# Down projection of the gated ConvFFN in a diffusion inference step: seven block products in place of eight

## The reference

```python
def conv_ffn(h, rows, cols, w_up, w_dw, b_dw, w_down):
    up = h @ w_up
    a, g = jnp.split(up, 2, axis=-1)
...
    g4 = lax.conv_general_dilated(g4, w_dw.reshape(3, 3, 1, D_FF).astype(g4.dtype), (1, 1), 'SAME',
                                  dimension_numbers=('NHWC', 'HWIO', 'NHWC'), feature_group_count=D_FF)
    g = g4.reshape(B, L, D_FF) + b_dw
    return (jax.nn.gelu(g) * a) @ w_down
...
    ffn = conv_ffn(h, rows, cols, p['w_up'], p['w_dw'], p['b_dw'], p['w_down'])
    x = layer_norm(ALPHA * x + g2[:, None, :] * ffn, p['ln2_g'], p['ln2_b'])
```

## Time and profile before

| | us |
|---|---|
| median of 3 runs | 1409.03 |
| lowest and highest | 1407.51, 1412.31 |
| the profiled execution: its own time | 1409.17 |
| its span from first to last instruction | 1407.4 |

### The profile page before, as it was taken

One profiled execution on the slowest core, in us unless ns is written; L12 is line 12 of the kernel. 1 busy time (PEld: TensorE's weight loads), 2 busy tenths in 40 slices (PEclk: granted clock), 3 DMA queues, 4 the chain that ended last, 5 costly groups with the idle time before them and its releaser, 6 DMA issues.

```text
span 1407.4 us, 22364 instructions
## 1 busy us (share of the span) xinstructions
PE 1308.3 (93%) x7871; PEld 1205.1 (86%) x7871; DVE 962.5 (68%) x1478; ACT 589.1 (42%) x1021; POOL 571.0 (41%) x432
## 2 busy tenths in 40 slices
PE   5899899889998799997899999999999999999995
PEld 3689899789988677897899999999999888788784
DVE  7565659673467688879877768677755655855846
ACT  5442124334345624454344444444434444343440
POOL 1002999333333121339566675766656610000000
PEclk9899999989999899999999999999999999999998
DMA  9432231463335432201231322223121496394771
GB/s 341 133 91 83 65 89 45 144 193 82 91 98 182 153 118 103 75 31 54 70 107 57 108 78 85 93 69 108 62 86 48 136 318 196 125 306 134 231 241 48
DMA packets 150412, 171.65 MB, mean 122 GB/s; under 512 B 9832, under 2 KB 109508, under 8 KB 150084
## 3 DMA queue, kind: packets, MB, share of 16 engines
q1 hardware_dynamic: 149854, 165.93, 37.2%
q0 software_dynamic: 288, 4.72, 0.8%
q10 hardware_dynamic: 197, 0.06, 0.0%
HBM read 142.88 MB, written 27.80 MB: 121 GB/s over the span
## 4 chain that ended last, share of the span: by engine, by line
PE 73%; DVE 13%; issue 4%; DMA 3%; ACT 3%; POOL 3%; SPq 0%; POOLq 0%; DVEq 0%; ACTq 0%
PE ps L1315 10%; PE ps L1313 10%; PE ps L1314 10%; PE ps L969 10%; PE ps L1349 6%; PE ps L1351 6%; PE ps L1350 6%; DVE qk L2346 2%; DVE aacc L2364 2%; PE ps L921 2%; DMA adaw<-in_w_ada 2%; PE ps L880 1%; PE ps L1189 1%; PE ps L1191 1%; PE ps L1190 1%
## 5 line engine op out<-in xcount | busy, mean ns | idle before, releaser
L2658 DVE SCALAR_TENSOR_TENSOR ps<-gs,taps,ps 128x945 f32<-128x945 f32 (+2 forms) x176 | 215.8, 1226 | 37.9 <-ACT ps L1736 32.4
L2036 POOL TENSOR_TENSOR rstd<-mv,neghalf 128x1 f32<-128x1 f32 x27 | 25.1, 931 | 340.1 <-DVE mv L2545 332.1
L969 PE MATMUL ps<-h1hi,whi 128*128 128x384 f32 x432 | 155.4, 360 | 0.0
L969 PE MATMUL ps<-h1lo,whi 128*128 128x384 f32 x432 | 147.9, 342 | 0.0
L969 PE MATMUL ps<-h1hi,wlo 128*128 128x384 f32 x432 | 147.8, 342 | 0.0
L1888 POOL TENSOR_TENSOR wlo<-raw,whi 128x512 fp32r<-128x512 f32 x50 | 74.3, 1488 | 76.3 <-ACT whi L1431 29.2
L1313 PE MATMUL ps<-thi,xhi 128*128 128x288 f32 x320 | 95.6, 299 | 4.3 <-issue 4.3
L1313 PE MATMUL ps<-thi,whi 128*128 128x288 f32 x320 | 94.2, 294 | 2.3 <-POOL wlo L1888 2.3
L1315 PE MATMUL ps<-thi,xlo 128*128 128x288 f32 x320 | 95.5, 298 | 0.0
L1314 PE MATMUL ps<-tlo,xhi 128*128 128x288 f32 x320 | 95.3, 298 | 0.0
L1315 PE MATMUL ps<-thi,wlo 128*128 128x288 f32 x320 | 94.4, 295 | 0.0
(11 more groups left out here) (404 smaller groups left out, 4022.1 us busy)
## 6 DMA issues: line engine op xcount, KB each, us to landing
raw<-in_w_down SPq DMA_DIRECT2D x132, 256.0 KB, 3.3
raw<-in_w_up SPq DMA_DIRECT2D x78, 256.0 KB, 3.3
u_rows<-ub SPq DMA_DIRECT2D x22, 576.0 KB, 2.9
ur<-u_rows SPq DMA_DIRECT2D x66, 192.0 KB, 3.5
adaw<-in_w_ada SPq DMA_DIRECT2D x24, 512.0 KB, 4.0
raw<-in_w_in SPq DMA_DIRECT2D x40, 256.0 KB, 4.2
...
```

What stands on the lines that cost most here:

```text
L969: last = mm(ps[:, bank, 0:GN], a[:, n % 2, k * P:(k + 1) * P], b[:, kk, grp(g)], start=(kk == 0 and a is whi and b is h1hi), stop=(kk == K ...
L2658: step(stt(a3[:, ro, co], g3[:, ri, ci], taps[:, tap:tap + 1], a3[:, ro, co], ALU.mult, ALU.add), 2 + m)
```

## The change

**Products.** The latent tokens are cut into halves of 512 (four token tiles each), the features into two halves of 11 tiles (`KF`), and the output columns into halves of 512. With A for u and B for `w_down` (A21: second token half, first feature half), the seven products in their order are: 1 (`D_U1`) A21 B11; 2 (`D_U2`) A22 B21; 3 (`D_S1`) S1 T1; 4 (`D_S2`) S2 T2; 5 (`D_S4`) S4 B22; 6 (`D_S3`) S3 T3; 7 (`D_U4`) A12 T4. The sums are S1 = A11 + A12, S2 = S1 - A21, S3 = A21 - A11, S4 = A22 - S2, T1 = B12 - B11, T2 = B22 - T1, T3 = B22 - B12, T4 = T2 - B21. A product is 11 steps, one for each feature tile; a step is 4 token tiles by 3 passes = 12 matmuls. The context tile is multiplied beside them: 6 more matmuls per step in product 1 (B11, B12), 3 more in products 2 and 5.

**Who does what.** VectorE forms all eight sums in SBUF (`s1` to `s4`, `t1` to `t4`), one instruction of 512 columns for each feature tile, and all low parts except the first four steps (`N_POOL_LO`) and the context's B12 parts (`xw_lo`), which are GpSimd's. The raw operands come through rings of four (`ARING`). A finished product leaves PSUM by a ScalarE copy (`copy_product`, `copy_ctx`) or a VectorE addition into the output rows `z` (`c11`, `u2`, `u5`, `c12`, `u3_c22`).

**Norm.** For token tile number i (order: context, 4 to 7, 0 to 3) GpSimd multiplies by the gate (`gate3`, 128x1024), VectorE adds the residual (`residual3`) and takes the statistics, GpSimd makes `rstd`, ScalarE normalises (`normalise3`), VectorE multiplies by the gain (`gain3`, 128x1024), and GpSimd adds the bias (`shift3`, 128x1024). In product 7 the last four steps (`N_TAIL`) run by token tile, and `last_part` joins each tile's last 512 columns.

```diff
-U_END = U_DOWN + NG * FT * 2
-GU = 2 * FT
-DRING = 8
-POOL_KT = 5
-USRING = 4
+KF = FT // 2
+KD = KF * 7
+ARING = 4
+N_POOL_LO = 4
+N_TAIL = 4
+UX = UC + P
...
+            for p in range(7):
+                ctx = p in (D_U1, D_U2, D_S4)
+                order = {D_U2: (2, 3, 0, 1), D_S1: (1, 2, 3, 0), D_S3: (1, 2, 3, 0)}.get(p, (0, 1, 2, 3))
+                for j in range(KF - N_TAIL if p == D_U4 else KF):
+                    ready(p, j)
+                    if ctx and j == KF - 1:
+                        ctx_mms(p, j)
+                    for i in order:
+                        if j == 0:
+                            bank_free(p, i)
+                        last = tile_mms(p, j, i)
+                    if ctx and j < KF - 1:
+                        last = ctx_mms(p, j)
+                    last.then_inc(pe_unit, 1)
+            for i in range(H):
+                for j in range(KF - N_TAIL, KF):
+                    if i == 0:
+                        ready(D_U4, j)
+                    last = tile_mms(D_U4, j, i)
+                last.then_inc(pe_zt, 1)
...
+            def u_hi(p, j):
+                m = KF * p + j
...
+                act.wait_ge(pe_unit, U_DOWN + max(m - 3, -4))
...
+            def gate3(i):
...
+                tt(row_, row_, grows2[:, who(t), :], ALU.mult).then_inc(zg_ready, 1)
+            def shift3(i):
...
+                tt(row_, row_, lnrows2[:, 1, :], ALU.add).then_inc(z_ready, 1)
...
+            def u_lo(p, j):
+                m = KF * p + j
+                dve.wait_ge(ushi_ready, m + 1)
+                ins = tt(u_split(ulo, p, j), u_source(p, j), u_split(uhi, p, j).bitcast(F32), ALU.subtract)
...
+            def s2(j):
+                dve.wait_ge(*x_landed(D_S1, j))
+                dve.wait_ge(*ulo_count(KF * D_S1 + j))
+                tt(su[j][:, :], su[j][:, :], x_part(D_S1, j), ALU.subtract).then_inc(s_formed, 1)
...
+            def residual3(i):
+                row_ = z[TILE_OF[i]][:, :]
+                dve.wait_ge(zg_ready, ZG_0 + i + 1)
+                dve.wait_ge(y_in[i % 3], 16 * (i // 3 + 1 + times(i % 3)))
+                stt(row_, zt[i % 3][:, :], ALPHA, row_, ALU.mult, ALU.add).then_inc(z_added, 1)
+                dve.wait_ge(z_added, ZA_0 + i + 1)
...
+            for j in range(N_POOL_LO):
+                t1(j)
+                s3(j)
+            conv(FT - 1, (FT - 1) % 2, lambda: both_lo(D_U1, N_POOL_LO))
+            both_lo(D_U1, N_POOL_LO + 1)
+            u_make(FT - 1, (FT - 1) % 2, UO_0 + 16 * (FT // 2 - 1))
...
+            last_part(5)
+            last_part(6)
+            neg_mean3(5)
+            gain3(5)
+            last_part(7)
```

More of the change, by code:

```diff
@@ new lines, in layer @@
+        uhi = place("uhi", [P, ARING, UX], dt=F32R)
+        dwhi = place("dwhi", [P, ARING, UC], dt=F32R)
+        assert top[0] <= u_at + big // 2
+        top[0] = u_at + big
+        ulo = place("ulo", [P, ARING, UX], dt=F32R)
+        dwlo = place("dwlo", [P, ARING, UC], dt=F32R)
+        assert top[0] <= u_at + big + big // 2
+        z_one, z_two = M0 + 4 * row, M0 + big + 4 * row
+        xw = [(place(f"xwhi{r}", [P, UC], z_one + 8 * UC * r, F32R), place(f"xwlo{r}", [P, UC], z_one + 8 * UC * r + 4 * UC, F32R))
+              for r in range(ARING)]
@@ new lines, in layer, with family @@
+        z = [place(f"z{t}", [P, DM], (z_two if t < H else z_one) + 4 * DM * (t % H)) for t in range(LT)]
+        z.append(place("z_ctx", [P, DM], M0 + big + 2 * row + 8 * UC))
+        def family(name, at, more, n):
+            return [place(f"{name}{j}", [P, UC], at + 4 * UC * j if j < n else more[0] + 4 * UC * (j - n)) for j in range(KF)]
+        su = family("su", u_at + big + big // 2, (M0,), 9)
+        tw = family("tw", u_at + big // 2, (M0 + big + 2 * row,), 9)
+        tw2 = family("tw2", u_at + 2 * big, (0,), KF)
@@ new lines, in ctx_mms @@
+            def ctx_mms(p, j):
+                m, other = (KF * p + j) % ARING, BANKS[1 - p % 2]
+                u = uhi[:, m, UC:UX], ulo[:, m, UC:UX]
+                if p == D_U1 and j == 0:
+                    pe.wait_ge(val_copied, V_0 + FT)
+                elif p == D_U2 and j == 0:
+                    pe.wait_ge(p_copied, PC_0 + 3)
+                elif p == D_S4 and j == 0:
+                    pe.wait_ge(down_used, 6)
+                last = three(ps[:, other[0], :], u, (dwhi[:, m, :], dwlo[:, m, :]), j == 0, j == KF - 1)
+                if p == D_U1:
+                    pe.wait_ge(xwlo_ready, XW_0 + j + 1)
+                    last = three(ps[:, other[1], :], u, [x[:, :] for x in xw[j % ARING]], j == 0, j == KF - 1)
+                if j == KF - 1:
+                    last.then_inc(pe_zt, 1)
+                return last
@@ L1811, in seven @@
                 acc_init(j + (N_PLAIN + jj), par)
+                if end:
+                    xw_hi(0)
                 formed(b, jj, 6)
@@ L1879, in _ @@
+            for i in range(5, NT):
+                normalise3(i)
         @block.gpsimd
@@ L2658, in conv @@
                     step(stt(a3[:, ro, co], g3[:, ri, ci], taps[:, tap:tap + 1], a3[:, ro, co], ALU.mult, ALU.add), 2 + m)
+                    if m == 4 and between is not None:
+                        between()
                 for dx in (-1, 1):
@@ new lines, in _ @@
+            for j in range(KF):
+                both_lo(D_S3, j)
+                if j == 2:
+                    ctx_add(D_S4, BANKS[1][0], 1)
+                if 3 <= j < 7:
+                    c12(j - 3)
+                if j == 4:
+                    residual3(0)
+                if j == 5:
+                    stats3(0)
+                if j == 6:
+                    residual3(1)
+                if j == 7:
+                    neg_mean3(0)
+                    stats3(1)
+                if j == 8:
+                    gain3(0)
+                    residual3(2)
+                if j == 9:
+                    neg_mean3(1)
+                    stats3(2)
+                if j == 10:
+                    gain3(1)
+                    residual3(3)
@@ new lines, in _ @@
+            last_part(5)
[3 more added lines that the diff above has]
+            last_part(7)
+            neg_mean3(6)
+            gain3(6)
+            last_part(8)
+            neg_mean3(7)
+            gain3(7)
+            neg_mean3(8)
+            gain3(8)
+            dve.wait_ge(zs_ready, ZN_0 + NT)
+            for half in range(2):
+                cols = slice(half * UC, (half + 1) * UC)
+                out = z[TILE_OF[NT - 1]][:, cols]
+                tt(out, out, lnrows2[:, 1, cols], ALU.add).then_inc(zl_ready, 1)
```

866 lines of the change are left out of this document (555 added, 311 removed).

## The result

The changed kernel takes **1416.69 us** (median of 7 runs, 1413.91 to 1423.91), the kernel before, run beside it, 1407.51 (median of 7, 1405.00 to 1413.54). The ratio is **1.0075**, with a 95% interval of 1.0048 to 1.0102. The profiled execution of after took 1413.91 us, its span is 1412.2. In it the down part begins 5.1 us earlier than in before's profile (1111.82 in place of 1116.95). Why is not known. So I compare spans from the first matmul of the down part to the end: 290.5 us before, 300.4 after, **9.9 us more**. The medians differ by 9.2.

What follows compares the result with a forecast made beforehand. Matmuls bound the kernel before; in products 6 and 7 VectorE becomes the bound. 239.4 matmuls + 4.7 product 1 + 25.2 waits + 0.4 clock + 19.8 tail = 289.5 against 290.45, giving 1408 us, range 1390 to 1418.

Steps and rivals of the forecast that it cites:

- Matmuls, 29.9 us saved: Down part: 1056 matmuls, 132 fewer than 1188, at 0.2267 us each, leaving 239.4 us.
- Product 1, 4.7 us: Product 1: 3.0 us of waits for low parts and sums plus 1.7 at the lower clock; ends 0 and 9.
- Products 2 to 5, covered: Products 2 to 5: VectorE, ScalarE and loads keep up, so they run at TensorE's pace, 134.6 us.
- VectorE's own load in products 6 and 7, 8.2 us of waits: Last low parts ready at 59.2 us, wanted at 51.0, so TensorE waits even with nothing in VectorE's way.
- The clock, 0.4 us: Products 6 and 7: TensorE's clock may fall during long waits; VectorE hides that except for some 0.4 us.
- GpSimd in VectorE's way: 17 us more: Products 6 and 7: 13 GpSimd passes, 32.5 us, 87% overlapped, cost VectorE 0.6 per us; ends 11.3 and 22.6.
- full blocking: Rival: VectorE passes with two SBUF operands stand still while GpSimd runs; 28.3 us for 17.0, time 1422; chance 0.12.
- Where the waits stand: Products 6 and 7: most of TensorE's 25.2 us of waits ahead of the last four steps, gap 8 us or more.
- hardly slowed: GpSimd's own passes were taken to be hardly slowed when they run beside VectorE's; about 2.5 us per 1024-column pass.
- The tail, 19.8: Behind the last matmul: norm and store take 19.8 us in place of 14.5; ends 16 and 23.
- No loss: Rival: GpSimd's and VectorE's passes do not meet or meet cheaply; 1387 us; chance 0.19 for below 1395.
- The clock rival: Products 6 and 7: TensorE falls to 1.2 GHz for good; last 39 matmuls 16.6 us, time 1416; chance 0.10.

Runs made afterwards that it cites:

- e8_first: Changed kernel with GpSimd's low parts in product 1 filled with zeros instead of formed from two operands, so left out of the product; 1412.44 us.
- e10_both: Changed kernel with last norm's gates, gain, bias on VectorE, partly moved earlier, and product 1's low parts ahead of earlier steps' sums; 1394.26 us, ratio 0.9921 to before.
- e1_thin: Changed kernel with GpSimd's gate and bias passes of the last norm cut from 1024 columns to one, every wait kept; 1386.69 us.

## Why the prediction was wrong, step by step

The forecast was 1408 us and no difference; it came out 1416.7, inside the range (1390 to 1418) and on the slower side, which had 0.26.

- **Matmuls, 29.9 us saved: right.** 1056 at 0.2267 us.
- **Product 1, 4.7 us: right in size (5.3), partly by luck.** The sum had 3.0 us of waits and 1.7 of lower clock. The granted clock was 1.00 throughout, and the waits were 5.3. The one ahead of step 6 (2.3) was there, and its cause was the one named (e8_first, e10_both); those for GpSimd's first low parts, given up to 1 us, took 2.0, and the 0.9 in step 8 was not foreseen.
- **Products 2 to 5, covered: right**, 134.64 us where 134.6 was worked out.
- **VectorE's own load in products 6 and 7, 8.2 us of waits: right** (8.2, e1_thin). The steps that it counts up to TensorE's need are 18, as its 51.0 us has them, and not "7 + 10".
- **The clock, 0.4 us: too small.** I said that VectorE would hide it but for this. It hides it up to the last low part; the 39 matmuls behind that start at 1.2 GHz (granted clock 0.50 ahead of them) and took 2.3 us more (0.79 over the 39). Not all of it reached the end: VectorE, whose passes lead to the end, waited for them once, 1.59 us at 1386.11.
- **"GpSimd in VectorE's way: 17 us more": this is the step that failed.** It measured 24.4 us of TensorE's waits (34.9 less 8.2 and 2.3), 25.0 on VectorE. That the passes meet was no error: all 13 that were counted did, and the context's gate besides. The price was: 0.6 us per us of overlap, taken between the 0.6 beside low parts and the 0.7 of the longest row, with ends of 0.4 and 0.8, on 28.3 us (87% of 32.5). On that scale the runs give 0.86, beyond the upper end. And it is no rate: over the 39.5 us that GpSimd was busy it is 0.63, and with the passes cut in four (63.1 us) 0.27. What is fixed is that a held pass of 512 columns ends 0.54 to 0.55 us behind the instruction that holds it. The rows for that stood in the earlier trace rows: the median 0.75 and the maximum 2.89 of one line fit two kinds of passes, free ones and ones held for a whole GpSimd instruction (after has the same pair, 0.69 and 2.74 to 2.90). In before's trace 62 of the 84 take 0.73 to 0.75 us, and the longest stands beside this pass of GpSimd and ends 0.55 us behind it:

```profile
168.96 2.89 DVE L2364 SCALAR_TENSOR_TENSOR aacc<-adaw,colv,aacc 128x512 f32<-128x512 f32 x1
...
168.56 2.74 POOL L1965 TENSOR_TENSOR qk<-poolB,qk 128x1024 f32<-128x1024 f32 x1
```

  I read them as the ends of a scatter, and gave the rival that says it plainly, full blocking, 0.12. Its mechanism is what the runs show, and 0.86 is past the 0.75 from which it was said to decide. Its time, 1422, was too high (28.3 for 24.4, and 22.4 for 20.7 in the tail), since statistics and passes with a PSUM operand run beside GpSimd for free.
- **Where the waits stand: wrong.** Most were to come ahead of the last four steps, in a gap of 8 us or more. In after 9.9 us are lost in product 6, 12.7 in the first seven steps of product 7, 10.0 within its last four and 2.3 to the clock; the longest gap, from one matmul's start to the next, is 4.9 us.
- **GpSimd "hardly slowed": wrong.** It is held in its turn: 2.8 us a pass on average in products 6 and 7 in place of 2.4, and in product 1 once 9.29 in place of 1.3.
- **The tail, 19.8: near** (20.7), with three held passes and three waits of 1.31 us for ScalarE in it. Two errors cancel in part: from the last low part (1380.04) VectorE needed 32.1 us and not 28.7, and TensorE, slower than forecast, covered 11.5 of them and not 8.9. e1_thin's 16.4 shows the 4 us given to the bias passes.
- **Rivals.** "No loss" was priced at 1387, and e1_thin took 1386.7; so near it is luck. Its whole is 272.4, where the forecast less 17 and 4 has 268.5, and its down part begins 4.4 us earlier than before's. The clock rival gave the last 39 matmuls 16.6 us, as if they all ran at the lower level; they took 11.3, so the higher one came back within them, as its counter-argument said.
- **Small slips.** Four gains of 2.4 us are 9.6, not 9.8; of the 22 passes of the earlier trace rows with a PSUM operand 21 lie beside GpSimd's work, not all. Neither changes anything.

The terms add up: 239.4 matmuls + 5.3 + 34.9 + 20.7 = 300.3, against the 289.5 forecast: 9.3 of the 10.8 too little lie in products 6 and 7, 7.4 of them in the one price, 1.9 in the clock.

The Trainium skill ("Advanced Engine Details and Errata", GPSIMD Details) says that GpSimd shares a read and a write interface with VectorE and conflicts with VectorE's instructions of two SBUF inputs, and the traces agree: passes with two SBUF operands are held, statistics and PSUM passes are not. The words "interfere/block" in its Mode Summary are said of VectorE's two-port modes; the forecast took them for passes with two SBUF operands. For these the traces show the blocking and give its unit, a whole instruction.
